# Gate columns as the stationary operand, the delta rule's output in two groups of four, and the stream 192 bytes further along

## The chip, the cores and the metric

The kernel runs on one core of one Trainium2 chip. The metric is device microseconds of one execution. Three runs of the kernel before took 1904.73, 1896.8 and 1905.82 us, so the median is 1904.73 us. Every profile row further down is from one more, profiled execution.

## The reference, cut to what matters

A model of four blocks works on one sequence of 256 tokens of width 1024, all in float32: two blocks of the first kind (L = 0, 1), then two of the second kind (L = 2, 3). The change touches the first kind alone, and there the mixer called the gated delta rule. From the reference:

```python
proj = h @ w_in
(dn_qkv, dn_z, dn_b, dn_a, ...) = jnp.split(proj, ...)   # dn_b, dn_a: 4 columns each
beta = jax.nn.sigmoid(dn_b)
g = -jnp.exp(dn_A_log) * jax.nn.softplus(dn_a + dn_dt_bias)

def step(state, inp):                   # one of 4 chunks of 64 tokens, 4 heads at once
    u_c, w_c, a_c, qd_c, kt_c, dl_c = inp
    v_new = u_c - jnp.einsum('bhck,bhkv->bhcv', w_c, state)
    o = jnp.einsum('bhck,bhkv->bhcv', qd_c, state) + jnp.einsum('bhcj,bhjv->bhcv', a_c, v_new)
    state = state * dl_c[..., None, None] + jnp.einsum('bhck,bhcv->bhkv', kt_c, v_new)
    return state, o
```

`h` is the RMS norm of the stream, so `dn_b` and `dn_a` are eight columns of the product of the stream with `w_in`, times one factor for each token. The output `o` of a chunk is the sum of two products for each head: one with the state, one with `v_new`. In the first chunk the state is zero and the first product falls away.

## The kernel before, in words

**Weights and the big products.** All weights come as 572 chunks of 128 partitions by 1024 columns. SyncE issues each chunk's DMA into a ring `raw`; ScalarE casts it to its high part `whi` (line 636); VectorE subtracts to get its low part `wlo` (line 1126, as part of `split`; GpSimd does some). The three rings hold four chunks each. The stream lies in two tiles: `hh` is its high part and `hl` its low part, each eight blocks of 256 tokens. A product of one weight block of 128x128 with the stream is three matmuls with 256 moving columns, `hh` with `whi`, `hl` with `whi` and `hh` with `wlo` (helper `mm3`). A chunk of `w_in` is 24 such matmuls. All matmuls are recorded at line 2001, in the helper `mm`; operands read in plain float32 need two passes each, shown as two records.

**The start of a block.** `first(L)` on TensorE opens with `project("qkv", L, ...)`, a generator that does one chunk for each `next`. In its hook, between chunk 3 and chunk 4 (counted from 0; the order's rows and the timeline show it behind a chunk in bank 5), it issues `norm_sum`, two plain float32 matmuls that sum squares; from these ScalarE makes `RSB`, the norm's factor along the free axis, and VectorE makes `RST`, the same factor with tokens on the partitions. After chunk 4 TensorE issues the gate columns: `SW` holds the eight columns of `w_in` for `dn_b` and `dn_a`, as 8 high and 8 low columns for each of eight blocks. ScalarE fills the high half (line 882) and VectorE the low half in their own hooks. The product goes to bank 1 with tokens on the partitions; VectorE copies the low half out (line 1451), adds the high half, and multiplies by `RST`. Then `beta` and the decays follow in a few 128x8 instructions of both engines. Beside this VectorE runs, for every chunk of qkv, one `wlo`, and for most of them one multiplication by `RSB` that empties a bank (128x512) and six steps of the convolution.

**The delta rule beside the weights.** `mixers` and `run` interleave the delta rule's steps with weight chunks of the same block (`fill`): a step of the small matmuls, one chunk, the next step. `delta(L)` writes the output of chunk n = 0..3, for heads of each half, into banks 2 and 3 by matmuls with 64 moving columns: `St` (the state, 128 rows by 128 columns) for n > 0 and `VN` (the new values, 64 rows by 128 columns). In the trace a name such as 64*128 ahead of the shape is the part of the array that the stationary operand fills: rows by columns. The four heads run in a loop, each with its `St` matmul and then its `VN` matmul. Ahead of them, in the same step, stand four matmuls of 64 rows (two passes each) for the state. There are two blocks with n = 0, and three with `St` in each of the two layers: six.

**Addresses.** The tiles lie one behind the other in the local memory: rings first, then constants, parameters, `small`, `RST`, then `hh`, `hl`, `RSB`, `SW` and the big `region` that holds nearly every other tile (`area`).

Of the kernel before, what the change touches and what calls it, by code (L numbers as in the profile page):

```python
# [7 lines left out]
F32 = mybir.dt.float32  # L8
# [47 lines left out]
                         ("dnout", 1), ("retout", 4), ("pscale", 4), ("alog", 8), ("dtb", 8)])  # L56
N_PAR2 = _columns(PAR2, [("attn", 8), ("mlp", 8), ("final", 8), ("idxk", 1), ("sinks", 8)])
N_PAR = DEPTH * (N_PAR1 + N_PAR2)
N_SMALL = 64 + 512


class Job:
# [120 lines left out]
def wide(ap, axis, n):  # L183

    shape = list(ap.shape)
    shape.insert(axis, n)
    return ap.unsqueeze(axis).broadcast_to(shape)
# [84 lines left out]
def program(nc, ins, out):  # L272
    with ExitStack() as ctx:
# [35 lines left out]
        def sb(name, shape, dt=F32, offset=None):  # L309
            n = 4  # L310
            for x in shape[1:]:
                n *= x
            if offset is None:
                offset = at[0]
                at[0] += (n + 31) // 32 * 32
            return nc.alloc_sbuf_tensor_at(name, shape, dt, offset=offset)
# [5 lines left out]
        cst = sb("cst", [P, N_CONST])  # L322
        par = sb("par", [P, N_PAR])
        small = sb("small", [P, N_SMALL])
        RST = sb("RST", [P, 2])
        hh = sb("hh", [P, 8, T], F32R)
        hl = sb("hl", [P, 8, T], F32R)
        RSB = sb("RSB", [P, T])
        SW = sb("SW", [P, 8, 16], F32R)
        region = at[0]  # L330
        nslots = (nc.sbuf_usable_end - region) // 4096
        assert nslots >= 30, nslots
        area = nc.alloc_sbuf_tensor_at("area", [P, 30 * 1024], F32, offset=region)

        def slot(i, n=1):
# [60 lines left out]
        a_, be, g_, eg, kx = (SM[:, 16 * i:16 * i + 8] for i in (0, 1, 2, 4, 5))  # L396
        G_, GL = SM[:, 48:56], SM[:, 56:64]
        u1, u2 = SM[:, 128:136], SM[:, 144:152]
        AB2, tmp2 = (SM[:, c:c + 16].rearrange("p (s c) -> p s c", s=2) for c in (192, 224))
        AB = SM[:, 192:208].rearrange("p (s c) -> p c s", s=2)  # L400
        sm3 = small[:, 0:64].rearrange("p (k c) -> p k c", c=8)

        QF = slot(0, 7)
# [208 lines left out]
        def scalar(a):  # L612
# [246 lines left out]
            def first(L):  # L859
# [18 lines left out]

                def hook():
                    factor(norm)  # L880
                    a.wait_ge(s_small[L], 16)
                    a.copy(SW[:, :, 0:8], sm3).then_inc(*a_dn.up("SW", L))

                def rv(m0):
                    a.wait_ge(*v_norm.at("turned", norm))
# [2 lines left out]
                qkv = project("qkv", L, conv, hook)  # L888
                next(qkv)
                next(qkv)  # L890
                next(qkv)
                next(qkv)
                a.wait_ge(*v_dn.at("ab", L))
# [230 lines left out]
        def vector(v):  # L1124
            def tt(dst, x, y, op):
                return v.tensor_tensor(dst, x, y, op)  # L1126
# [291 lines left out]
            def first(L):  # L1418
# [19 lines left out]

                def hook():
                    factor(norm)  # L1440
                    v.wait_ge(*a_dn.at("SW", L))
                    tt(SW[:, :, 8:16], sm3, SW[:, :, 0:8].bitcast(F32), OP.subtract).then_inc(*v_dn.up("SW", L))

                qkv = project("qkv", L, conv, hook, norm)
                next(qkv)
                next(qkv)
                next(qkv)
                next(qkv)
                two = bank[1][:, 0:32].rearrange("p (s c) -> p s c", s=2)
                v.wait_ge(*e_dn.at("ab", L))  # L1450
                v.tensor_copy(tmp2, two[:, :, 8:16]).then_inc(*v_dn.up())
                v.wait_ge(*v_dn.now())
                tt(AB2, two[:, :, 0:8], tmp2, OP.add).then_inc(*v_dn.up("absum", L))
                v.wait_ge(*v_dn.now())
                v.wait_ge(*v_norm.at("turned", norm))
                tt(AB2, AB2, wide(RST[:, :], 2, 8), OP.mult).then_inc(*v_dn.up("ab", L))
                v.wait_ge(*v_dn.now())

                dn = delta(L)
# [530 lines left out]
        def tensor(e):  # L1990
# [9 lines left out]
            def mm(ps, x, y, start, stop, skip=False):  # L2000
                return e.matmul(ps, x, y, start=start, stop=stop, skip_group_check=skip)  # L2001
# [248 lines left out]
            def fresh2(b0, event):  # L2250
                for j in range(2):
                    fresh(b0 + j, event(j))

            def delta(L):
# [74 lines left out]
                for n in range(4):  # L2329
# [18 lines left out]
                    if n == 0:  # L2348
                        e.wait_ge(*g_dn.at("q", L))
                        fresh2(2, lambda j: a_dn.at("OD", L, j))  # L2350
                    for h in range(4):
                        b = 2 * h + half
                        o = bank[2 + h // 2][:, 256 * (h % 2) + 64 * n:256 * (h % 2) + 64 * n + 64]
                        if n:
                            mm(o, St[:, 128 * h:128 * h + 128], Aq[:, 256 * h + 64 * n:256 * h + 64 * n + 64], True, False)
                        x = mm(o, hv(VN)[r, h, :], AT[r, 128 * b + 64 * q:128 * b + 64 * q + 64], n == 0, True)
                    x.then_inc(*e_dn.up("o", L, n))
                    yield 1
                e.wait_ge(*a_dn.at("square", L))
# [89 lines left out]
            def first(L):  # L2449
# [9 lines left out]
                next(qkv)  # L2459
                next(qkv)  # L2460
                next(qkv)
                next(qkv)
                e.wait_ge(*v_dn.at("SW", L))
                fresh(1, v_dn.at("absum", L))
                for s in range(2):
                    for k in range(8):
                        mm(bank[1][:, 16 * s:16 * s + 16], hh[:, k, 128 * s:128 * s + 128], SW[:, k, :], k == 0, False, True)
                        x = mm(bank[1][:, 16 * s:16 * s + 8], hl[:, k, 128 * s:128 * s + 128], SW[:, k, 0:8], False, k == 7, True)
                x.then_inc(*e_dn.up("ab", L))
                dn = delta(L)  # L2470
                next(dn)
# [282 lines left out]
def parameters(inputs):  # L2754
# [4 lines left out]
    for l in range(DEPTH):  # L2759
# [17 lines left out]
        put(PAR2, par2, "sinks", x["sinks_2"][l].reshape(2, 2, 2).transpose(0, 2, 1).reshape(1, 8))  # L2777
        small[l][:, 0:64] = x["w_in"][l][:, 2048:2056].reshape(8, P, 8).transpose(1, 0, 2).reshape(P, 64)
        small[l][:, 64:576] = x["pool_w"][l].transpose(1, 0, 2).reshape(P, 512)
    return par1, par2, small  # L2780


# [32 lines left out]
```

## Time and profile before

| what | value |
|---|---|
| median of three runs | 1904.73 us |
| the profiled execution's own time | 1908.99 us |
| its span | 1907.2 us |
| mean granted TensorE clock | 0.993 |
| TensorE busy (PE) | 1879.3 us, 99% |
| VectorE busy (DVE) | 1246.2 us, 65% |
| ScalarE busy (ACT) | 955.7 us, 50% |
| GpSimd busy (POOL) | 308.5 us, 16% |
| chain that ended last | PE 90%, DVE 7%, ACT 1%, DMA 1% |

Busy shares are of the whole span, and the chain's shares tell which engine the end waited for. A granted clock of 1.00 is 2.4 GHz on TensorE, one of 0.50 is 1.2 GHz; a mean between them is a stretch with some of each.

### The profile page before, as it was taken

How to read it: one execution, taken by the hardware profiler on the slowest of the kernel's cores; microseconds unless marked ns; L12 is line 12 of the kernel's file. 1: busy time of each engine (PE TensorE's matmuls, PEld its weight loads, DVE VectorE, ACT ScalarE, POOL GpSimd, SP SyncE). 2: the span in 40 equal slices, each digit the busy share in tenths (PEclk: the TensorE clock that was granted, in tenths of full speed). 3: DMA queues.
4: the chain of work that ended last, by engine and by line, in shares of the span. 5: the costliest groups of instructions: out<-in, count | busy, mean ns of one | idle time of the engine just before them, and what ended most of it. 6: DMA issues, size and time to landing. Idle time of an engine off the chain costs nothing.

```text
span 1907.2 us, 36402 instructions
## 1 busy us (share of the span) xinstructions
PE 1879.3 (99%) x15460; PEld 1791.1 (94%) x15460; DVE 1246.2 (65%) x1678; ACT 955.7 (50%) x1381; POOL 308.5 (16%) x176
## 2 busy tenths in 40 slices
PE   7999999999999999999999999999999999999998
PEld 7989998998899999999989999999999899999998
DVE  6884567665689545877658775577547684677643
ACT  5633456544563435564445445555534444556533
POOL 0050231000003203200002342320001352321000
PEclk9999999999999999999999999999999999999999
DMA  6443344655445323555565553355555663345553
GB/s 228 161 145 111 120 146 159 211 187 198 145 154 178 110 97 127 200 181 182 193 209 184 178 179 131 123 188 193 187 186 179 211 195 121 132 167 188 190 187 100
DMA packets 92161, 317.59 MB, mean 167 GB/s; under 512 B 11744, under 2 KB 12896, under 8 KB 91744
## 3 DMA queue, kind: packets, MB, share of 16 engines
q1 hardware_dynamic: 91424, 314.69, 48.9%
q8 instruction: 123, 2.02, 0.4%
q10 hardware_dynamic: 576, 0.57, 0.1%
q14 instruction: 38, 0.31, 0.0%
HBM read 304.99 MB, written 1.05 MB: 160 GB/s over the span
## 4 chain that ended last, share of the span: by engine, by line
PE 90%; DVE 7%; ACT 1%; DMA 1%; issue 1%; SPq 0%; DVEq 0%; ACTq 0%
PE bank L2001 89%; DVE wlo L1126 3%; DVE area L1126 2%; PE bank L2543 1%; DVE area L1132 1%; DMA raw<-in_weights 1%; DVE hl L1132 1%; DVE xT L1132 1%; ACT area L630 1%; ACT whi L636 0%; PE bank L2561 0%; PE bank L2220 0%; DVE area L1196 0%; DVE xT L1126 0%; DVE area L1645 0%
## 5 line engine op out<-in xcount | busy, mean ns | idle before, releaser
L1126 DVE TENSOR_TENSOR wlo<-raw,whi 128x1024 fp32r<-128x1024 f32 x518 | 659.9, 1289 | 399.1 <-ACT whi L636 398.6
L2001 PE MATMUL bank<-hh,whi 128*128 128x256 f32 x2928 | 835.3, 286 | 15.8 <-DVE wlo L1126 13.1
L2001 PE MATMUL bank<-hh,wlo 128*128 128x256 f32 x2928 | 818.6, 281 | 0.0
L2001 PE MATMUL bank<-hl,whi 128*128 128x256 f32 x2928 | 811.7, 281 | 0.0
L636 ACT CAST whi<-raw 128x1024 fp32r<-128x1024 f32 x572 | 589.0, 1046 | 412.3 <-PE bank L2001 361.2
L2001 PEld LDWEIGHTS bank<-hh,whi 128*128 128x128 f32 x2928 | 555.7, 190 | 30.0 <-DVE wlo L1126 14.7
L2001 PEld LDWEIGHTS bank<-hl,whi 128*128 128x128 f32 x2928 | 555.8, 191 | 1.9 <-issue 1.9
L2001 PEld LDWEIGHTS bank<-hh,wlo 128*128 128x128 f32 x2928 | 556.2, 190 | 0.0
L1781 POOL TENSOR_TENSOR area<-area 128x512 f32<-128x512 f32 (+4 forms) x86 | 137.4, 1604 | 559.3 <-ACT area L630 219.4
L1781 POOL TENSOR_TENSOR wlo<-raw,whi 128x1024 fp32r<-128x1024 f32 x54 | 134.0, 2483 | 426.3 <-ACT whi L636 426.3
L2001 PE MATMUL bank<-area 64*64 64x64 f32 (+7 forms) x1928 | 184.9, 268 | 0.7 <-DVE area L1196 0.7
L2001 PEld LDWEIGHTS bank<-area 64*64 64x64 f32 (+3 forms) x1928 | 163.9, 168 | 18.3 <-issue 6.9
L2001 PE MATMUL bank<-FH,whi 128*128 128x256 f32 x640 | 180.1, 281 | 0.0
L2001 PE MATMUL bank<-FL,whi 128*128 128x256 f32 x640 | 179.6, 281 | 0.0
L2001 PE MATMUL bank<-FH,wlo 128*128 128x256 f32 x640 | 179.6, 281 | 0.0
L630 ACT ACTIVATE area<-area 128x256 f32<-128x256 f32 (+8 forms) x247 | 140.7, 578 | 50.6 <-DVE area L1132 18.6
L2001 PEld LDWEIGHTS bank<-FL,whi 128*128 128x128 f32 x640 | 122.3, 191 | 0.1
L2001 PEld LDWEIGHTS bank<-FH,whi 128*128 128x128 f32 x640 | 120.1, 188 | 0.4 <-issue 0.3
L2001 PEld LDWEIGHTS bank<-FH,wlo 128*128 128x128 f32 x640 | 120.5, 188 | 0.0
L1126 DVE TENSOR_TENSOR area<-bank,area 128x512 f32<-128x512 f32 (+4 forms) x146 | 83.0, 610 | 42.9 <-PE bank L2001 39.5
L1126 DVE TENSOR_TENSOR area<-bank,RSB 128x512 f32<-128x512 f32 (+1 forms) x118 | 80.2, 682 | 44.1 <-PE bank L2001 41.4
L2001 PE MATMUL bank<-wlo,FH 128*128 128x512 f32 x240 | 94.8, 395 | 0.0
(129 smaller groups left out, 1915.5 us busy)
## 6 DMA issues: line engine op xcount, KB each, us to landing
raw<-in_weights SPq DMA_DIRECT2D x572, 512.0 KB, 4.1
area<-area SPq DMA_DIRECT2D x96, 64.0 KB, 3.5
area<-area SPq DMA_DIRECT2D x16, 128.0 KB, 3.8
cst<-in_const SPq DMA_DIRECT2D x1, 1188.0 KB, 7.3
cst<-in_const SPq DMA_DIRECT2D x1, 1024.5 KB, 5.5
xT<-in_x SPq DMA_DIRECT2D x4, 256.0 KB, 8.0
out<-xT SPq DMA_DIRECT2D x4, 256.0 KB, 2.9
area<-in_lev SPq DMA_DIRECT2D x2, 384.0 KB, 6.6
```

The costliest lines, as they stand in the source:

```text
L630: return a.activation(dst, src, fn, scale=scale, **more)
L636: a.copy(whi[:, i % RING, :], raw[:, i % RAW, :]).then_inc(*hi.up(i))
L1126: return v.tensor_tensor(dst, x, y, op)
L1132: return v.scalar_tensor_tensor(out=dst, in0=x, scalar=s, in1=y, op0=op0, op1=op1)
L1781: return g.tensor_tensor(dst, x, y, op)
L2001: return e.matmul(ps, x, y, start=start, stop=stop, skip_group_check=skip)
L2543: o = e.transpose(bank[b][:, 128 * u:128 * u + 128], x.grid()[:, j % 2, j // 2, 128 * kb:128 * kb + 128], C("eye"))
```

## The change: what it does

**Gate columns.** `SW` becomes the stationary operand and the stream the moving one: 16 matmuls (8 blocks, one with `hh` and 16 columns of `SW`, one with `hl` and 8) with 256 moving columns, instead of 32 with 16 or 8. They stand behind `norm_sum` and ahead of chunk 4. The result has the eight columns on partitions 0 to 15 and tokens along the free axis. VectorE copies it (16x256) to `ABR`. After chunk 4 TensorE turns it back with two plain float32 matmuls against a small matrix of two stacked 8x8 identities, which comes with `small` and also adds the high and low halves. VectorE then needs one instruction, the multiplication by `RST`, where it had three. The cast and the subtraction that fill `SW` move one weight chunk earlier on ScalarE and VectorE.

**Output.** For n > 0 the four `St` matmuls stand ahead of the four `VN` matmuls.

**Addresses.** `small` grows by 32 bytes for each partition, `RST` moves behind the region, and a gap is put in, so that `hh`, `hl`, `RSB`, `SW` and the region begin 192 bytes further along in each partition. The rings keep their addresses.

The diff, with unchanged lines left out:

```diff
-N_SMALL = 64 + 512
+N_SMALL = 64 + 512 + 8
...
-        RST = sb("RST", [P, 2])
+        at[0] += 192
         hh = sb("hh", [P, 8, T], F32R)
...
-        nslots = (nc.sbuf_usable_end - region) // 4096
+        at[0] += 30 * 4096
+        RST = sb("RST", [P, 2])
...
+        ABR = SM[0:16, 0:256]
...
@@ ScalarE, first block
                 def hook():
                     factor(norm)
-                    a.wait_ge(s_small[L], 16)
-                    a.copy(SW[:, :, 0:8], sm3).then_inc(*a_dn.up("SW", L))
...
                 next(qkv)
                 next(qkv)
+                a.wait_ge(s_small[L], 16)
+                a.copy(SW[:, :, 0:8], sm3).then_inc(*a_dn.up("SW", L))
...
@@ VectorE, first block
                 def hook():
                     factor(norm)
-                    v.wait_ge(*a_dn.at("SW", L))
-                    tt(SW[:, :, 8:16], sm3, SW[:, :, 0:8].bitcast(F32), OP.subtract).then_inc(*v_dn.up("SW", L))
+                    v.wait_ge(*e_dn.at("abrow", L))
+                    v.tensor_copy(ABR, bank[1][0:16, 0:256]).then_inc(*v_dn.up("abrow", L))
...
                 next(qkv)
                 next(qkv)
+                v.wait_ge(*a_dn.at("SW", L))
+                tt(SW[:, :, 8:16], sm3, SW[:, :, 0:8].bitcast(F32), OP.subtract).then_inc(*v_dn.up("SW", L))
                 next(qkv)
                 next(qkv)
-                two = bank[1][:, 0:32].rearrange("p (s c) -> p s c", s=2)
                 v.wait_ge(*e_dn.at("ab", L))
-                v.tensor_copy(tmp2, two[:, :, 8:16]).then_inc(*v_dn.up())
-                v.wait_ge(*v_dn.now())
-                tt(AB2, two[:, :, 0:8], tmp2, OP.add).then_inc(*v_dn.up("absum", L))
-                v.wait_ge(*v_dn.now())
                 v.wait_ge(*v_norm.at("turned", norm))
-                tt(AB2, AB2, wide(RST[:, :], 2, 8), OP.mult).then_inc(*v_dn.up("ab", L))
+                tt(AB2, bank[1][:, 256:272].rearrange("p (s c) -> p s c", s=2), wide(RST[:, :], 2, 8), OP.mult).then_inc(*v_dn.up("ab", L))
...
@@ TensorE, delta
+                    def place(h):
+                        return bank[2 + h // 2][:, 256 * (h % 2) + 64 * n:256 * (h % 2) + 64 * n + 64]
+                    if n:
+                        for h in range(4):
+                            mm(place(h), St[:, 128 * h:128 * h + 128], Aq[:, 256 * h + 64 * n:256 * h + 64 * n + 64], h % 2 == 0, False, True)
                     for h in range(4):
                         b = 2 * h + half
-                        o = bank[2 + h // 2][:, 256 * (h % 2) + 64 * n:256 * (h % 2) + 64 * n + 64]
-                        if n:
-                            mm(o, St[:, 128 * h:128 * h + 128], Aq[:, 256 * h + 64 * n:256 * h + 64 * n + 64], True, False)
-                        x = mm(o, hv(VN)[r, h, :], AT[r, 128 * b + 64 * q:128 * b + 64 * q + 64], n == 0, True)
+                        x = mm(place(h), hv(VN)[r, h, :], AT[r, 128 * b + 64 * q:128 * b + 64 * q + 64], n == 0, True, True)
...
@@ TensorE, first block
                 next(qkv)
+                e.wait_ge(*v_dn.at("SW", L))
+                fresh(1, v_dn.at("ab", L))
+                for k in range(8):
+                    mm(bank[1][0:16, 0:T], SW[:, k, :], hh[:, k, :], k == 0, False, True)
+                    x = mm(bank[1][0:8, 0:T], SW[:, k, 0:8], hl[:, k, :], False, k == 7, True)
+                x.then_inc(*e_dn.up("abrow", L))
                 next(qkv)
-                e.wait_ge(*v_dn.at("SW", L))
-                fresh(1, v_dn.at("absum", L))
+                e.wait_ge(*v_dn.at("abrow", L))
                 for s in range(2):
-                    for k in range(8):
-                        mm(bank[1][:, 16 * s:16 * s + 16], hh[:, k, 128 * s:128 * s + 128], SW[:, k, :], k == 0, False, True)
-                        x = mm(bank[1][:, 16 * s:16 * s + 8], hl[:, k, 128 * s:128 * s + 128], SW[:, k, 0:8], False, k == 7, True)
+                    x = mm(bank[1][:, T + 8 * s:T + 8 * s + 8], ABR[:, 128 * s:128 * s + 128], small[0:16, 576:584], True, True)
                 x.then_inc(*e_dn.up("ab", L))
...
+        small[l][0:16, 576:584] = np.tile(np.eye(8, dtype=np.float32), (2, 1))
```

How the instructions move, at the three places that matter. In these rows a matmul's names are bank<-stationary and moving tile in the order of the alphabet, and the shape is that of its output; the number at a name tells tiles apart. First TensorE behind `norm_sum`, which is the row with `cst`, before:

```order
L2001 MATMUL bank5<-hh_57,wlo_52 128x256
L2001 MATMUL bank0<-area_61,cst_53 128x128 x2
L2001 MATMUL bank6<-hh_57,whi_51 128x256
L2001 MATMUL bank6<-hl_58,whi_51 128x256
L2001 MATMUL bank6<-hh_57,wlo_52 128x256
...
L2001 MATMUL bank1<-SW_60,hh_57 128x16
L2001 MATMUL bank1<-SW_60,hl_58 128x8
```

and after:

```order
L2002 MATMUL bank5<-hh_56,wlo_52 128x256
L2002 MATMUL bank0<-area_61,cst_53 128x128 x2
L2002 MATMUL bank1<-hh_56,SW_59 16x256
L2002 MATMUL bank1<-hl_57,SW_59 8x256
...
L2002 MATMUL bank1<-small_55,area_61 128x8 x2
```

The gate columns moved from behind chunk 4 (bank 6) to ahead of it, and their output lies turned; only the two small matmuls stay behind chunk 4. Next VectorE at the same place, before:

```order
L1126 TENSOR_TENSOR wlo<-raw,whi 128x1024 x3
L1126 TENSOR_TENSOR area<-RSB,cst 128x256
L1190 TENSOR_REDUCE RST<-area 128x2
L1126 TENSOR_TENSOR SW<-small,SW 128x8x8
L1126 TENSOR_TENSOR area<-bank,RSB 128x512 x2
...
L1126 TENSOR_TENSOR wlo<-raw,whi 128x1024
L1451 COPY area<-bank 128x16
L1126 TENSOR_TENSOR area<-bank,area 128x16
L1126 TENSOR_TENSOR area<-area,RST 128x16
L1126 TENSOR_TENSOR area<-area,par 128x8
```

and after:

```order
L1130 TENSOR_TENSOR wlo<-raw,whi 128x1024 x2
L1130 TENSOR_TENSOR SW<-small,SW 128x8x8
L1130 TENSOR_TENSOR wlo<-raw,whi 128x1024
L1130 TENSOR_TENSOR area<-RSB,cst 128x256
L1194 TENSOR_REDUCE RST<-area 128x2
L1446 COPY area<-bank 16x256
L1130 TENSOR_TENSOR area<-bank,RSB 128x512 x2
...
L1130 TENSOR_TENSOR wlo<-raw,whi 128x1024
L1130 TENSOR_TENSOR area<-bank,RST 128x16
L1130 TENSOR_TENSOR area<-area,par 128x8
```

The subtraction moved one `wlo` earlier, the new copy stands in its old place, and two of three small instructions are gone. Last the output step of the delta rule on TensorE in layer 0 with n > 0 (banks 2 and 3 take the outputs, bank 1 the state's part), before:

```order
L2001 MATMUL bank1<-area_61 128x128 x4
L2001 MATMUL bank2<-area_61 128x64 x4
L2001 MATMUL bank3<-area_61 128x64 x4
L2001 MATMUL bank6<-hh_57,whi_51 128x256
```

and after:

```order
L2002 MATMUL bank1<-area_61 128x128 x4
L2002 MATMUL bank2<-area_61 128x64 x2
L2002 MATMUL bank3<-area_61 128x64 x2
L2002 MATMUL bank2<-area_61 128x64 x2
L2002 MATMUL bank3<-area_61 128x64 x2
L2002 MATMUL bank6<-hh_56,whi_51 128x256
```

The same eight matmuls: before, `St` and `VN` by turns within each row of four; now the first two rows are `St` and the last two `VN`.

## Rows read from the trace of the kernel before

**Rows 1.** The page: busy time; the chain that ended last; a group (count | busy, mean ns).

```profile
PE 1879.3 (99%) x15460; PEld 1791.1 (94%) x15460; DVE 1246.2 (65%) x1678; ACT 955.7 (50%) x1381; POOL 308.5 (16%) x176
PE 90%; DVE 7%; ACT 1%; DMA 1%; issue 1%; SPq 0%; DVEq 0%; ACTq 0%
...
L2001 PE MATMUL bank<-hh,whi 128*128 128x256 f32 x2928 | 835.3, 286 | 15.8 <-DVE wlo L1126 13.1
```

**Rows 2.** The chain in order of time: start us, length us, what.

```profile
20.00 48.48 PE bank L2001 x375
...
149.90 66.78 PE bank L2001 x540
...
554.48 1.24 DVE wlo L1126
...
618.17 17.15 PE bank L2001 x220
```

**Rows 3.** Stretches, TensorE: us, PE busy (records), granted clock, DMA share, GB/s.

```profile
27.98:31.88 3.90, 3.90 (x34) 0.89 1.00 402
31.88:37.79 5.91, 5.91 (x29) 0.50 0.36 119
528.54:532.03 3.49, 3.49 (x34) 1.00 0.30 119
532.03:536.03 4.00, 4.00 (x23) 0.60 0.41 137
```

**Rows 4.** TensorE's timeline, both layers' norm_sum: start us, length us, engine, line, operation.

```profile
24.71 0.60 PE L2001 MATMUL bank<-area,cst 128*128 128x128 f32 x4
...
525.64 0.35 PE L2001 MATMUL bank<-hh,whi 128*128 128x256 f32 x1 [0.66 <-DVE wlo L1126]
```

**Rows 5.** VectorE's timeline, same columns, layer 0 and then layer 1.

```profile
26.77 0.42 DVE L1190 TENSOR_REDUCE RST<-area 128x2 f32<-128x256 f32 x1
27.10 0.22 DVE L1126 TENSOR_TENSOR SW<-small,SW 128x64 fp32r<-128x64 f32 x1
...
32.56 0.17 DVE L1451 COPY area<-bank 128x16 f32<-128x16 f32 x1
32.77 0.17 DVE L1126 TENSOR_TENSOR area<-bank,area 128x16 f32<-128x16 f32 x1
...
37.38 0.69 DVE L1126 TENSOR_TENSOR area<-bank,RSB 128x512 f32<-128x512 f32 x1 [0.76 <-PE bank L2001]
...
45.22 0.68 DVE L1126 TENSOR_TENSOR area<-bank,RSB 128x512 f32<-128x512 f32 x1
...
51.35 0.68 DVE L1126 TENSOR_TENSOR area<-bank,RSB 128x512 f32<-128x512 f32 x1
...
55.20 2.36 DVE L1126 TENSOR_TENSOR wlo<-raw,whi 128x1024 fp32r<-128x1024 f32 x2 [0.30 <-ACT whi L636]
...
536.67 0.69 DVE L1126 TENSOR_TENSOR area<-bank,RSB 128x512 f32<-128x512 f32 x1 [0.37 <-PE bank L2001]
```

**Rows 6.** Stretches, TensorE: output steps and what follows them.

```profile
165.97:167.89 1.92, 1.92 (x17) 1.00 0.61 203
174.87:179.62 4.75, 4.75 (x25) 0.81 0.29 110
179.62:184.88 5.26, 5.26 (x25) 0.52 0.27 90
188.83:192.83 4.00, 4.00 (x26) 1.00 0.36 128
690.00:692.00 2.00, 2.00 (x11) 0.50 0.00 0
692.00:694.00 2.00, 2.00 (x13) 0.69 0.42 137
```

**Rows 7.** Stretches, TensorE: two stretches of 40 us at full clock.

```profile
400.00:440.00 40.00, 40.00 (x342) 1.00 0.55 185
900.00:940.00 40.00, 40.00 (x355) 1.00 0.57 191
```

More of the change, by code:

```diff
@@ L330, in program @@
         region = at[0]
-        nslots = (nc.sbuf_usable_end - region) // 4096
-        assert nslots >= 30, nslots
+        at[0] += 30 * 4096
+        RST = sb("RST", [P, 2])
+        assert at[0] <= nc.sbuf_usable_end, at[0]
         area = nc.alloc_sbuf_tensor_at("area", [P, 30 * 1024], F32, offset=region)
@@ L398, in program @@
         u1, u2 = SM[:, 128:136], SM[:, 144:152]
-        AB2, tmp2 = (SM[:, c:c + 16].rearrange("p (s c) -> p s c", s=2) for c in (192, 224))
+        AB2 = SM[:, 192:208].rearrange("p (s c) -> p s c", s=2)
         AB = SM[:, 192:208].rearrange("p (s c) -> p c s", s=2)
+        ABR = SM[0:16, 0:256]
         sm3 = small[:, 0:64].rearrange("p (k c) -> p k c", c=8)
```

## The prediction, made before the changed kernel ran

> **What bounds the kernel now.** I read the page first. TensorE is busy for 99% of the span, and the chain that ended last runs over it for 90% and over VectorE for 7% [rows 1]. So work taken from TensorE is worth its length where the chain lies on TensorE, and nothing where it lies on VectorE. The chain in order of time says which is where [rows 2]. The output steps of the delta rule lie between 165 and 204 us and between 674 and 702 us, inside chain pieces of TensorE (149.90 to 216.68 in layer 0, and from 618.17 on in layer 1). There each microsecond counts. In the qkv product the chain is named as TensorE from 20.00 to 68.48, but this needs a second look: in layer 1 at the same place it goes over a `wlo` of VectorE at 554.48. In layer 0 the same `wlo` pair starts at 55.20 and takes 2.36 us [rows 5], so its first half ends at about 56.4, and TensorE takes the chunk that needs it at about that time. Both engines arrive together there, and whichever is faster gains nothing alone.
>
> Third, the granted clock. Behind the gate columns it fell to half: 0.50 over 5.91 us in layer 0, 0.60 over 4.00 us in layer 1 [rows 3]. It also fell behind two of the six output steps: 0.81 and 0.52 over 4.75 and 5.26 us, and 0.50 and 0.69 over two times 2 us [rows 6]. The loss in a stretch is its length times one minus its clock. That gives 0.43 + 2.96 = 3.4 us and 1.6 us for the gate columns, and 0.90 + 2.52 = 3.4 us and 1.0 + 0.62 = 1.6 us behind the output steps: 10.0 us in all.
>
> **The gate columns on TensorE.** Before: 32 matmuls. In layer 1, at full clock, they took 3.49 us [rows 3], 0.109 us each although they move only 16 or 8 columns; so the 128-column load of `hh` or `hl` sets the pace. After: 16 matmuls with 256 moving columns. At 40/355 = 0.113 us each [rows 7] this is 1.8 us. A stationary tile of 16 columns is a new shape; entering and leaving one costs, and two float32 matmuls (four passes, about 0.11 each) follow chunk 4. I add 0.9 us. So TensorE's own work falls by 3.5 − 2.7 = 0.8 us, and with the half clock gone by 0.8 + 3.4 = 4.2 us in layer 0 and 0.8 + 1.6 = 2.4 us in layer 1. In layer 1 the new block also fills time in which TensorE sat idle: 0.66 us ahead of chunk 4 [rows 4], which makes 3.1 us. I expect the clock to stay up because what preceded the fall is gone: 3.5 us of matmuls that are nearly all loading. What I can't exclude is that it falls anyway.
>
> The Trainium skill, in "TensorE: Matmul & The Clock Gate", section "LDWEIGHTS (loading the stationary operand)", says that a load takes columns divided by 1.2 ns, 107 ns for 128. The trace agrees: 109 ns in a run of matmuls that move next to nothing [rows 3]. By it the new loads of 16 columns would be 13 ns, and the 256 moving columns alone would set the pace, as my 1.8 us has it.
>
> **The gate columns on VectorE, which decides what of this is paid out.** From 38 us on VectorE is in a loop: two chunks in 51.35 − 45.22 = 6.13 us [rows 5], against 48 x 0.113 = 5.4 us on TensorE. TensorE has no lead to spend; if it comes earlier it waits for `wlo`. So what counts is by how much VectorE's loop starts earlier. Its wait for TensorE's bank, 0.76 us in layer 0 and 0.37 us in layer 1, goes, since chunk 4 and the next come earlier. Two small instructions go: 32.77 − 32.56 = 0.21 us each, 0.42. The `SW` subtraction moves into a time where VectorE waits anyway (behind the `wlo` of that chunk it has nothing to do until ScalarE's `RSB` comes), and in its place stands the new copy of 16x256. No row shows this shape. Its bounds: 0.17 us (a copy of 128x16) and 0.42 us (the reduction with 256 columns, both [rows 5]), against 0.22 us for the subtraction that leaves; I take 0.35, nearer to the row with the same 256 columns, so 0.13 to 0.2 us more than before. The copy must wait for the 16 matmuls. `norm_sum` starts at 24.71 [rows 4] and its four passes are through by 25.1, so they end at 25.1 + 2.0 = 27.1 us, and the reduction ahead of the copy ends at 27.2, so no new wait, but only by a tenth. In layer 1 the room is larger, since the block starts while chunk 4 still waits. Sum: layer 0 0.76 + 0.42 − 0.25 = 0.93 us, layer 1 0.37 + 0.42 − 0.2 = 0.59 us; together **1.5 us**. Its bounds are 0 (the copy waits and eats it) and 4.2 + 3.1 = 7.3 us (VectorE doesn't bind after all). Behind qkv the float chain of `beta` has only become shorter.
>
> **The output steps.** One with `St` takes 4.00 us for 24 records of its own at full clock; the one without `St` (n = 0) takes 1.92 us for 16 [rows 6]. The 8 more passes at 0.109 us are 0.87 us; the other 2.08 − 0.87 = 1.21 us are what the eight changes between a tile of 128 rows and one of 64 rows cost, 0.15 us each. Grouped there are two changes instead of eight: 6 x 0.15 = 0.9 us for a step, and six steps make **5.4 us**; I take 5.3, rounded down because the changes between matmuls of one step may hide a little in each other. It is in chain pieces of TensorE, and VectorE and ScalarE have idle time there. Bounds: 0 (the change of bank or of tile costs the same as the change of rows) and 6 x 1.21 = 7.3 us.
>
> The Trainium skill, in "TensorEngine Tiling (Array Packing)", section "Tiling Modes", says that changing the mode drains TensorE while changing the tile doesn't. The trace agrees, with 0.15 us for a change. The rule would put the same price on the new 16-column block, which I have in the 0.9 us above.
>
> **The clock behind the output steps.** It fell behind two of six steps in this execution and cost 5.0 us. The steps become a fifth shorter and denser. That can spare the falls, or none, or put one elsewhere. I take half, **2.5 us**, with bounds of 0 and 5.0.
>
> **Addresses.** No row shows what 192 bytes do. From below and above I take what the trace has at one clock for the same instructions: 342 matmul records in 40 us in one stretch and 355 in another [rows 7], 0.117 and 0.1127 us each, 4%. I take 0 and keep this for a rival. The Trainium skill, in "SBUF — State Buffer", section "Specifications (TRN2)", gives lines of 16 bytes, and 192 is twelve of them, so by that rule nothing changes; no run here shows it yet.
>
> **The sum.** 1.5 + 5.3 + 2.5 = 9.3 us from 1908.99 us gives 1899.7. The median of the runs is 4.3 us below the profiled execution, and the lowest 12 us. I suppose that a median run has lost less by half clock, so that only 1.3 of the 2.5 us can be saved there: 1904.73 − 1.5 − 5.3 − 1.3 = 1896.6. I say 1896.5.
>
> **Rivals.**
> 1. VectorE doesn't bind in qkv, or all falls of the clock go: the full 7.3 us in qkv, or 5.3 + 1.5 + 5.0. From the median 6.8 + 5.8 or 6.8 + 5.0, about 1892. For it: TensorE is called the chain in all of 20.00 to 68.48 [rows 2]. Against it: the period of 6.13 us.
> 2. Only the six steps pay, and the falls of the clock come back elsewhere: 5.3 or less, about 1900. For it: the two falls behind output steps came at only two of six like places, so what sets them off isn't just the step itself. In that case the clock would also fall in qkv, behind other work.
> 3. The order of the outputs saves nothing, because a new stationary tile costs the same whichever its rows: 1904.73 − 1.5 − 1.3, about 1902. Against it: n = 0 has 16 passes in 1.92 us, each with a tile of its own.
> 4. Slower: TensorE's pace for 256 moving columns depends on where the stream lies. The same matmul has two paces in this trace. There are 3 x 2928 of them with the stream's tiles [rows 1], about 8,800; if a third of all ran at 0.117 where they now run at 0.1127, it would be 2930 x 0.0043 = 12.6 us, and 1904.73 − 8.1 + 12.6 = 1909; with a half, 1915.5. It decides from about 1900 matmuls on, which is 8.1/0.0043. For it: the two paces are there at one clock. Against it: both are there with one placement, so placement alone does not set them.
>
> **Chances.** The forecast 0.42, rival 1 0.20, rival 2 0.20, rival 3 0.07, rival 4 0.11. The likeliest alone spans 1893 to 1900. The range reaches to rival 1 with a run-to-run spread of some microseconds below it, and to rival 3 above: 1887 to 1906. About 0.5%, 9.5 us, is what a measurement can tell here; that is below 1895.2 and above 1914.3. Rival 1 and half of the forecast's width lie below: 0.40. Of rival 4 about 0.08 lies above. The rest is 0.52.
>
> **What would show it.** Right: 16 records with a stationary of 16 columns right behind `norm_sum`, in about 2 us; a clock of 1.00 from 25 to 40 us and from 525 to 540 us; VectorE without a wait for TensorE's bank near 37 us, its next loop starting 0.9 us (0.6 us in layer 1) earlier; TensorE with small waits for `wlo` between 40 and 56 us; output steps of 3.1 us instead of 4.00. Wrong: VectorE waiting for the new copy's matmuls; TensorE a full 4 us ahead at 68 us; output steps that still take 4 us; or 40 us stretches whose record counts differ from 342 and 355 at places that the change doesn't touch, which would be rival 4.

## The result, and the profile after

The changed kernel took 1927.76 us, the median of four runs from 1927.51 to 1930.07 us; the kernel before took 1905.28 us, the median of four from 1896.8 to 1909.77. The ratio is 1.0115, with a 95% interval of 1.0082 to 1.0148: some 22 us slower, where 8 us faster were forecast. The profiled execution took 1927.51 us against 1908.99. One later run of the kernel before, among those made beside the first address experiments, took 2311.37 us against 1892 to 1915 us for the other 18, and the ratios there leave it out.

The page after, in the same lines as [rows 1]: busy time, the chain that ended last, and the costliest group of matmuls.

```profile
PE 1897.3 (99%) x15436; PEld 1808.5 (94%) x15436; DVE 1250.8 (65%) x1676; ACT 957.1 (50%) x1381; POOL 303.7 (16%) x176
...
PE 90%; DVE 6%; ACT 2%; DMA 1%; issue 1%; SPq 0%; DVEq 0%; ACTq 0%
...
L2002 PE MATMUL bank<-hh,whi 128*128 128x256 f32 x2928 | 839.8, 288 | 16.3 <-DVE wlo L1130 12.8
```

TensorE is busy for 18 us more, with 24 records fewer, so it takes longer over what it had before. The mean duration of a matmul on the page hardly shows it (288 against 286 ns), since matmuls are pipelined. The distance between their starts shows it. Here are two starts that lie 24 matmuls apart, in the middle of a long stretch at full clock, first of the kernel before and then of the changed one (timeline: start us, length us, engine, operation):

```profile
909.79 0.28 PE L2001 MATMUL bank<-hh,whi 128*128 128x256 f32 x1
...
912.51 0.28 PE L2001 MATMUL bank<-hh,whi 128*128 128x256 f32 x1
```

```profile
909.79 0.28 PE L2002 MATMUL bank<-hh,whi 128*128 128x256 f32 x1
...
912.64 0.28 PE L2002 MATMUL bank<-hh,whi 128*128 128x256 f32 x1
```

That is 2.72/24 = 113.3 ns before and 2.85/24 = 118.8 ns after. The place shown ran at the faster of two paces before. The kernel has 11,748 matmuls with 256 moving columns and 128x128 weights. Over the whole trace, the starts of successive ones lie 116.0 ns apart in the mean before, in two paces, about two fifths at 113.3 and three fifths at 117.8 ns. After, they lie 118.9 ns apart, most at 118.7 and about a quarter at 120.0 ns. So both kernels have two paces, and in the changed one both are slower.

What the change was forecast to do where it was made, it did. TensorE's and then VectorE's timeline after, layer 0:

```profile
23.34 0.61 PE L2002 MATMUL bank<-area,cst 128*128 128x128 f32 x4
23.70 0.36 PE L2002 MATMUL bank<-hh,SW 128*16 128x256 f32 x1
...
25.65 0.28 PE L2002 MATMUL bank<-hh,whi 128*128 128x256 f32 x1
```

```profile
25.40 0.42 DVE L1194 TENSOR_REDUCE RST<-area 128x2 f32<-128x256 f32 x1
25.85 0.41 DVE L1446 COPY area<-bank 16x256 f32<-16x256 f32 x1
...
35.06 0.68 DVE L1130 TENSOR_TENSOR area<-bank,RSB 128x512 f32<-128x512 f32 x1
...
52.86 2.36 DVE L1130 TENSOR_TENSOR wlo<-raw,whi 128x1024 fp32r<-128x1024 f32 x2 [0.30 <-ACT whi L640]
```

The 16 matmuls take 25.65 − 23.70 = 1.95 us, the copy 0.41, and the wait of 0.76 us for TensorE's bank [rows 5] is gone at 35.06. The stretches of TensorE (us, PE busy, granted clock, DMA share, GB/s), three output steps and the places where the clock had fallen [rows 3, 6]:

```profile
174.60:177.76 3.16, 3.16 (x26) 1.00 0.52 166
184.85:188.00 3.15, 3.15 (x26) 1.00 0.48 160
195.10:198.26 3.16, 3.16 (x26) 1.00 0.54 167
30.00:40.00 10.00, 10.00 (x86) 1.00 0.56 203
170.00:190.00 20.00, 20.00 (x158) 1.00 0.31 103
530.00:540.00 10.00, 10.00 (x85) 1.00 0.32 107
680.00:700.00 20.00, 20.00 (x158) 1.00 0.40 132
```

All six output steps fell to 3.16 us, from 4.00 at full clock, and at the places where the clock had fallen it now stays full. So where is the loss? The chain after, in order of time, has it at two marks:

```profile
552.11 1.24 DVE wlo L1130
...
616.73 17.34 PE bank L2002 x220
```

At 616.73 us the changed kernel is still 1.44 us ahead of [rows 2] (618.17). Then one and the same small block of the third layer, before and after:

```profile
1101.69 1.26 PE L2001 MATMUL bank<-area 64*128 64x128 f32 x12
```

```profile
1106.07 1.26 PE L2002 MATMUL bank<-area 64*128 64x128 f32 x12
```

It is 4.38 us behind there and 1925.7 − 1907.2 = 18.5 us behind at the end. Those last 14 us arise in a part of the program in which the change has not one instruction. Only the addresses differ there.

### The profile page after: what moved, and what is told of

Read it like the earlier page. It is cut to its first block, busy times and chain, and to the rows that moved or that the text cites. A ratio compares the mean times of both kernels' runs of the same rounds, so it can differ in the third digit from the quotient of the medians.

```text
span 1925.7 us, 36352 instructions
## 1 busy us (share of the span) xinstructions
PE 1897.3 (99%) x15436; PEld 1808.5 (94%) x15436; DVE 1250.8 (65%) x1676; ACT 957.1 (50%) x1381; POOL 303.7 (16%) x176
## 4 chain that ended last, share of the span: by engine, by line
PE 90%; DVE 6%; ACT 2%; DMA 1%; issue 1%; SPq 0%; DVEq 0%; ACTq 0%
PE bank L2002 89%; DVE wlo L1130 2%; DVE area L1130 1%; ACT area L634 1%; PE bank L2554 1%; DVE area L1136 1%; DVE hl L1136 1%; DVE xT L1136 1%; ACT whi L640 1%; DMA xT<-in_x 0%; DMA raw<-in_weights 0%; DVE area L1646 0%; PE bank L2221 0%; DVE area L1644 0%; PE bank L2572 0%
## 5 line engine op out<-in xcount | busy, mean ns | idle before, releaser
L2002 PEld LDWEIGHTS bank<-hl,whi 128*128 128x128 f32 x2928 | 548.9, 189 | 1.9 <-issue 1.9
L1782 POOL TENSOR_TENSOR area<-area 128x512 f32<-128x512 f32 (+4 forms) x86 | 132.9, 1550 | 569.5 <-ACT area L634 224.3
L2002 PE MATMUL bank<-area 64*64 64x64 f32 (+7 forms) x1928 | 179.2, 267 | 0.7 <-DVE area L1200 0.7
L1130 DVE TENSOR_TENSOR area<-bank,area 128x512 f32<-128x512 f32 (+3 forms) x144 | 82.6, 615 | 46.8 <-PE bank L2002 42.4
```

Of the source, the lines that this page charges most:

```text
L1782: return g.tensor_tensor(dst, x, y, op)
```

## The experiments

**Four parts, one by one.** All four ran on one chip beside 29 runs of the kernel before (median 1911.09 us).

The changed kernel without its gap:

```diff
-        at[0] += 192
         hh = sb("hh", [P, 8, T], F32R)
```

> The changed kernel with the gap of 192 bytes taken out, so that stream, SW and region lie where they lay before; gate columns and output order as changed. Placement theory (TensorE's pace for 256 moving columns is set by where the moving tiles lie): the paces of before come back (342 to 355 records in the 40 us stretches from 400 and from 900 us, against 340 and 339 in the changed kernel), and the time is the one before less 1.5 us in qkv, 5.0 us for the output steps and up to 10 us of half clock: 1889 to 1899 us. History theory (the new instructions themselves, by their order, leave TensorE in the slower pace): it stays within 3 us of 1927.8 us.

Measured: ratio to the kernel before 0.9964 (0.9939 to 0.9990), median 1904.51 us of 12 runs from 1886.85 to 1908.38. In its profiled execution (1886.85 us, the fastest) the mean pace is 115.2 ns and the clock is 0.999. Its counts in the 40 us stretches were 336 and 293, not the 342 to 355 expected. That says nothing of the pace: this execution is so far ahead that 19 and 62 of the matmuls in these stretches are others, with 512 moving columns and about 230 ns each, and the rest start 113.3 ns apart. From here on I read starts. The median lies above the 1889 to 1899 us expected, and the kernel before was slower on this chip too (1911.09 us for 1905.28). The rest of the change is a gain of 0.36%, and the gap turned it into a loss.

The kernel before with the gap alone:

```diff
+        at[0] += 192
         hh = sb("hh", [P, 8, T], F32R)
```

> The kernel before with nothing but a gap of 192 bytes ahead of the stream. Placement theory: about 11,400 matmuls take 119 instead of 116 ns each, so 33 us more, 1938 us, or down to 1928 if the falls to half clock go as they did in the changed kernel; 340 records or fewer in each 40 us stretch. History theory: no change, 1900 to 1909 us.

Measured: 1.0173 (1.0138 to 1.0208), median 1941.27 us; 1.0173 of 1905 is 33 us more. Two starts 24 matmuls apart:

```profile
909.77 0.28 PE L2002 MATMUL bank<-hh,wlo 128*128 128x256 f32 x1
...
912.65 0.28 PE L2002 MATMUL bank<-hh,wlo 128*128 128x256 f32 x1
```

2.88/24 = 120.0 ns; the mean of the trace is 119.2. That is what the placement theory said, within some 3 us (the medians differ by 30 us, the ratio makes 33), and the history theory (no change) falls.

The output steps alone:

```diff
+                    if n:
+                        for h in range(4):
+                            mm(place(h), St[...], Aq[...], h % 2 == 0, False, True)
                     for h in range(4):
                         b = 2 * h + half
-                        o = bank[2 + h // 2][...]
-                        if n:
-                            mm(o, St[...], Aq[...], True, False)
-                        x = mm(o, hv(VN)[r, h, :], AT[...], n == 0, True)
+                        x = mm(place(h), hv(VN)[r, h, :], AT[...], n == 0, True, True)
```

> The kernel before with only the output steps regrouped (St four times, then VN four times). Both theories: each of the six steps takes 3.16 us instead of 4.00, 5.0 us less in all, and no change of pace; 1900 us, or down to 1895 if the falls to half clock behind output steps go too. If the history theory holds in the form that the order of outputs matters for what follows, the pace behind these steps turns to 0.119 us and the time rises to 1915 or more.

Measured: 0.9963 (0.9936 to 0.9989), median 1899.82 us: 7 us less. And the gate columns alone (the diff is the changed kernel's, without the part on `place` and without the gap):

> The kernel before with only the gate columns as the stationary operand; output steps and addresses as before. Placement theory: 0.9 us in layer 0 and 0.6 us in layer 1 from VectorE's earlier loop, and the clock stays up behind the gate columns; since VectorE binds there, this pays nothing more: 1903.8 us, or down to 1898 if the falls behind the output steps go as well. History theory: the new block leaves TensorE in the slower pace, 1915 us or more.

Measured: 1.0005 (0.9979 to 1.0031), median 1912.01 us: no gain that can be told, and the 1.5 us expected are too small for this interval to show or exclude. Stretches of TensorE, of the gate columns alone and then of the output steps alone:

```profile
170.00:180.00 10.00, 10.00 (x65) 0.86 0.23 73
180.00:190.00 10.00, 10.00 (x64) 0.80 0.30 106
190.00:200.00 10.00, 10.00 (x53) 0.66 0.16 53
690.00:700.00 10.00, 10.00 (x65) 0.83 0.15 52
30.00:40.00 10.00, 10.00 (x89) 1.00 0.55 199
```

```profile
30.00:40.00 10.00, 10.00 (x75) 0.83 0.57 202
520.00:530.00 10.00, 9.34 (x71) 0.87 0.57 185
170.00:180.00 10.00, 10.00 (x82) 1.00 0.30 105
180.00:190.00 10.00, 10.00 (x81) 1.00 0.30 107
690.00:700.00 10.00, 10.00 (x79) 1.00 0.33 109
```

With the new gate columns the clock stays up behind them and falls behind output steps, for 1.4 + 2.0 + 3.4 + 1.7 = 8.5 us in this one execution, more than in the profile before (5.0). With the new output steps the falls behind them are gone, and those behind the gate columns stay, smaller than before (3.4 us for 5.0); by the prediction's argument VectorE's loop hides most of their cost, which no run tests. One execution is little to go by, since the falls differ from run to run. Over all runs the mean clock is 0.9943 for the kernel before (29 runs), 0.9957 with the gate columns alone, 0.9966 with the output steps alone, and 0.9987 with both (12 runs each). So with the gate columns alone a part of what they save may come back behind output steps, and the two gains of clock together (0.0014 + 0.0023) are most of what both parts bring (0.0044). Only with both parts is it 0.998 or 0.999 in all 12 runs.

**Whose address counts?** These two ran on one chip together with the gaps of 64 and 128 bytes further down (median before 1906.81 us). First the 192 bytes ahead of the rings, so that rings and stream move together:

```diff
+        at[0] += 192
         raw = sb("raw", [P, RAW, 1024])
...
-        at[0] += 192
         hh = sb("hh", [P, 8, T], F32R)
```

> The changed kernel, but the 192 bytes are put ahead of the weights' rings, so that rings, constants, stream and region all lie 192 bytes further and no distance between them differs from before. If what counts is how the moving tile lies relative to the stationary one (distance theory), TensorE has the two paces of before, 113.3 and 117.8 ns, and the time is that of the changed instructions at the old addresses, 1887 to 1908 us, median 1904. If the moving tile's own address counts (own-address theory), the matmuls keep their mean of 119 ns and the time is 1925 to 1930 us.

Measured: 0.9941 (0.9910 to 0.9972), median 1895.44 us. Two starts 24 matmuls apart:

```profile
909.80 0.28 PE L2002 MATMUL bank<-hh,whi 128*128 128x256 f32 x1
...
912.52 0.28 PE L2002 MATMUL bank<-hh,whi 128*128 128x256 f32 x1
```

113.3 ns again, with the stream at the very address at which the changed kernel had it. So the distance between stream and weights counts, not the stream's own place. Next the gap behind `SW`, for the region alone (one run):

```diff
-        at[0] += 192
         hh = sb("hh", [P, 8, T], F32R)
...
+        at[0] += 192
         region = at[0]
```

> The changed kernel with the gap of 192 bytes behind SW: only the region (with FH and FL, the moving tiles of w_down, 1920 matmuls of 256 columns) lies further, the stream hh and hl where it lay before. Both placement theories: matmuls with hh and hl have the paces 113.3 and 117.8 ns, those with FH and FL 119 to 120; so about 1920 x 2 to 3 ns = 4 to 6 us more than with no gap, 1891 to 1910 us. If the region alone did it (through other engines' tiles in it), all matmuls take 119 ns and the time is 1927 us.

Measured: 1906.7 us. Counted over the whole trace, matmuls with `hh` and `hl` as the moving tile come 115.6 ns apart, in the paces 113.3 and 117.8; those with `FH` and `FL` come 118.7 ns apart. Each class follows its own tile. One run of a kernel whose fellows spread over 20 us says nothing by its time; the paces do, and they exclude that the region's place slows all matmuls.

**The distance, step by step.** Only the number in `at[0] += 192` was changed. The gaps of 256, 32 and 224 bytes ran on a third chip (median before 1902.38 us). The rings' tiles begin at multiples of 256 bytes, so the last bits of `hh`'s address are the distance modulo 256.

> The changed kernel with a gap of 64 bytes in place of 192. Placement theory with a pattern that repeats: hh begins at 88064, which is 0 modulo 256, as the rings do; no trace so far shows this residue. If equal residues of moving and stationary tile are the bad case, and 192 (residue 128) is only half bad, it is slower than 1928 us, up to 1950. If the farther from the residue of before (192) the worse, then 64 lies between: 1905 to 1928. If only lines of 16 bytes counted, it would be as with no gap, 1887 to 1908.

> The changed kernel with a gap of 128 bytes in place of 192; hh begins at 88128, residue 64 modulo 256. By symmetry with the residue of before (192 and 64 lie equally far from the rings' residue 0) the two paces of before would come back: 1887 to 1908 us. If each step of 64 bytes from the old place only makes it worse, it is at 1920 to 1928.

> The changed kernel with a gap of 256 bytes in place of 192: the stream lies again 192 bytes, modulo 256, behind the rings, as before. Distance theory with a period of 256 bytes: the paces 113.3 and 117.8 ns come back and the time with them, 1887 to 1908 us. If the period is longer (512 or more) or the distance itself counts, the pace stays at 118 to 120 ns and the time is 1915 to 1935 us.

> The changed kernel with a gap of 32 bytes: residue 224 of 256, between those of no gap (192) and of a gap of 64 (0, every matmul at 120.0 ns). If the pattern goes in steps of 64 bytes, it is like one of its neighbours: 1887 to 1908 us or 1934. If it changes smoothly, between: 1910 to 1925. Lines of 16 bytes alone would give no difference from no gap.

> The changed kernel with a gap of 224 bytes: residue 160 of 256, between that of the changed kernel (128, 1928 us) and of no gap (192, 1887 to 1908 us). Steps of 64 bytes: as at 192, 1928 us, or as with no gap. Smooth: between, 1905 to 1920 us, with matmuls of 115 to 118 ns.

| gap, bytes | distance mod 256 | ratio to before | 95% interval | mean pace, profiled run |
|---|---|---|---|---|
| 0 | 192 | 0.9964 | 0.9939 to 0.9990 | 115.2 ns |
| 32 | 224 | 1.0081 | 1.0056 to 1.0106 | 118.3 ns |
| 64 | 0 | 1.0126 | 1.0090 to 1.0162 | 119.9 ns |
| 128 | 64 | 1.0038 | 1.0018 to 1.0058 | 117.5 ns |
| 192 (the change) | 128 | 1.0115 | 1.0082 to 1.0148 | 118.9 ns |
| 224 | 160 | 1.0089 | 1.0060 to 1.0119 | 118.2 ns |
| 256 | 192 | 0.9951 | 0.9917 to 0.9985 | 115.7 ns |
| 192, rings too | 192 | 0.9941 | 0.9910 to 0.9972 | 115.4 ns |

Gaps of 0 and 256 agree, so the pattern repeats after 256 bytes. Distance 0 is the slowest of these, as one of the expectations had it. Distance 64 came out at 117.5 ns: nearly always the slower of the two paces that 192 has, so my "by symmetry" was half right. The gaps of 32 and 224 bytes give 118.3 and 118.2 ns. That is at no neighbour's value, so the step form is out. Both lie between their neighbours, nearer to the slower one: gap 32 came out inside the smooth form's range (1922.11 us of 1910 to 1925), gap 224 just outside it (1921.80 us of 1905 to 1920).

The profiled executions of the eight placements in the table tie pace to time. A straight line through them, from 115.2 ns and 1886.85 us to 119.9 ns and 1935.09 us, rises by 10.4 us for each nanosecond, and none lies more than 3 us off it. All 11,748 matmuls on the critical path would make 11.7 us for each.

**TensorE alone.** To measure the disputed cost by itself:

```diff
+ORDER = [p for _ in range(5) for k in range(8) for p in ((k, k), (k, 8 + k), (8 + k, k))]
...
+            x = [e.matmul(bank[1][:, 0:T], st(k, 0), mv(j, 192), start=i == 0, stop=i == 119, skip_group_check=True) for i, (k, j) in enumerate(ORDER)][-1]  # stationary 0, moving 192
+            x.then_inc(s_pe, 1)
+            e.wait_ge(s_v, 2)
```

> A kernel that computes nothing of the model: after one copy of x into a stationary tile S and a moving tile M, TensorE alone runs 38 blocks of 120 matmuls (128x128 stationary, 256 moving, float32r, in the order high-high, high-low, low-high), each pair of blocks at another start address of M, with S at 0 or 64 modulo 256; between blocks VectorE copies one bank, nothing else runs and no transfer is under way. Distance theory (TensorE's own two reads, of the stationary and of the moving tile, get in each other's way, by the distance of their addresses modulo 256): a block at distance 192 takes 120 x 113.3 to 117.8 ns = 13.6 to 14.1 us, at 0 it takes 120 x 120 = 14.4, at 64 14.1, at 128 14.2 to 14.4, at 32, 160 and 224 between; and with S at 64, M at 0 behaves as 192 did and M at 64 as 0. Rival (other engines' or transfers' accesses to the same memory slow TensorE down): with nothing beside it, every block takes the same, 13.6 us or less. Rival (own address of the moving tile counts): with S at 64 the blocks behave by M's residue as with S at 0.

The timeline, one block of 120 matmuls to a row (start us, length us). In order: distances 192, 224, 0, 64 twice, 128, 192 once more twice; then, with the stationary tile at 64, the moving tile at 0 and at 64.

```profile
53.90 13.88 PE L325 MATMUL bank<-M,S 128*128 128x256 f32 x120 [0.52 <-DVE xT L308]
68.30 14.47 PE L328 MATMUL bank<-M,S 128*128 128x256 f32 x120 [0.52 <-DVE xT L308]
98.26 14.66 PE L334 MATMUL bank<-M,S 128*128 128x256 f32 x120 [0.52 <-DVE xT L308]
...
158.18 13.87 PE L346 MATMUL bank<-M,S 128*128 128x256 f32 x120 [0.52 <-DVE xT L308]
172.57 14.40 PE L349 MATMUL bank<-M,S 128*128 128x256 f32 x120 [0.52 <-DVE xT L308]
...
217.83 14.50 PE L358 MATMUL bank<-M,S 128*128 128x256 f32 x120 [0.52 <-DVE xT L308]
...
277.77 13.89 PE L370 MATMUL bank<-M,S 128*128 128x256 f32 x120 [0.52 <-DVE xT L308]
292.17 14.40 PE L373 MATMUL bank<-M,S 128*128 128x256 f32 x120 [0.52 <-DVE xT L308]
...
456.67 13.89 PE L406 MATMUL bank<-M,S 128*128 128x256 f32 x120 [0.52 <-DVE xT L308]
...
485.47 14.64 PE L412 MATMUL bank<-M,S 128*128 128x256 f32 x120 [0.52 <-DVE xT L308]
```

No other engine works during a block, and transfers are at 1 GB/s or less. Still the same differences come out: 14.66 − 13.88 = 0.78 us for 120 matmuls between distances 0 and 192, or 6.5 ns each, against 119.9 − 113.3 = 6.6 ns in the full kernel. A block's length holds its slower start too. In its middle the starts lie 113.3 ns apart at 192, 118.3 at 224, 120.0 at 0, 118.7 at 128, and 113.3 or 117.8 at 64: the full kernel's paces. With the stationary tile at 64 the two values change places as the distance says: the moving tile at 0 now takes 13.89 us and at 64 it takes 14.64. Both rivals, other engines' accesses and the moving tile's own address, are out as what sets these paces. And the same distance, 192 as well as 64, gave 13.9 us in one block and 14.4 in another. The output bank isn't what differs: at 192 the blocks at 53.90 and 292.17 us both write bank 4. Distances 160, 208 and 16 had two lengths as well (14.51 and 14.35, 14.56 and 14.27, 14.51 and 14.27 us), and distance 96, which no full kernel had, was as slow as 0 (14.65 us). So the pace doesn't follow the distance in a smooth line. This kernel ran once.

## Why the prediction was wrong

**The step that failed is the one on addresses: "I take 0 and keep this for a rival".** Its cost is 33 us when it is alone (1.0173), and 1.0115/0.9964 = 1.0152, or 29 us, beside the other parts. Rival 4 had the right mechanism (TensorE's pace depends on where the stream lies) and a price of 12.6 to 19 us. That was too low, because it counted only a share of the matmuls turning from the fast pace of before to its slow one; in fact nearly all went to paces that the trace of before does not have, 118.7 and 120.0 ns. It also counted 3 x 2928 matmuls, those with `hh` and `hl`, where some 11,700 of this form had their moving tile shifted. Its own evidence was misread too. I held against it that both paces appear with one placement, so that placement alone doesn't set them. That is true, and it excluded nothing: placement sets which paces there are, and something else picks between two of them. Rows 7, read as a bound, gave the difference within one distance and no bound for another distance.

The Trainium skill was used for the same step ("SBUF — State Buffer", section "Specifications (TRN2)", lines of 16 bytes, of which 192 bytes are a whole number). The measurement decides against that use, that a shift by whole lines changes nothing: gaps of 32, 64 and 128 bytes are whole numbers of such lines as well, and they moved the time by 0.7 to 1.6% against no gap. In "TensorE: Matmul & The Clock Gate", section "Step-by-step: what each phase is for", it also says that loading the next tile's weights takes no read bandwidth from the running matmul. TensorE alone doesn't fit that: its pace changes by up to 6.5 ns a matmul with the distance between the two tiles. That the two reads get in each other's way is the reading I take; the runs show the dependence on the distance and not what happens inside.

**The gate columns on TensorE: right.** 1.95 us for the 16 matmuls, where 1.8 was said, and the clock stayed up, here and with the gate columns alone.

**What VectorE pays out: right, nearly to the digit.** From the instruction that reads `RSB` to the `wlo` pair that TensorE then waits for it was 55.20 − 26.31 = 28.89 us in layer 0 and is 52.86 − 24.94 = 27.92; in layer 1 554.48 − 525.97 = 28.51 and now 552.11 − 524.18 = 27.93. That is 0.97 + 0.58 = 1.55 us, forecast 1.5. The new copy took 0.41 us, not 0.35, and found its matmuls done.

**The output steps: right in kind, a little large.** 6 x 0.84 = 5.0 us against 5.3.

**The clock behind them: under-valued, and its cause not seen.** Half of the falls behind output steps were forecast to go. In the profiles of seven of the eight placements with both parts all went, in that at a gap of 64 bytes one was left (a clock of 0.83 from 680 to 690 us). With the gate columns alone they went behind these and grew behind the output steps, which is like rival 2; with the output steps alone they went behind these and stayed in part behind the gate columns. In time the parts add up as far as this can be told: 0.9963 x 1.0005 = 0.9968 alone, 0.9964 together, each with about 0.0026 either way. The argument that took 1.3 us for the 2.5, that a median run of the kernel before has lost less by half clock, is not borne out: of 29 runs the fastest (1893.37 us) and the slowest (1917.83) both have a mean clock of 0.993.

**The sum without the gap: right, and in part by luck.** The forecast was 8.1 us below the median, 0.43%; the change without its gap measured 0.36% (0.10 to 0.61). Three placements of the changed kernel at distance 192 beat both kernels, at 0.9941 to 0.9964. But the interval reaches from 2 to 12 us, and the terms didn't come out as summed: 1.55 + 5.0 us for the instructions, and up to 5.0 us behind the output steps where 1.3 was taken.

**What stays open.** What picks between the two paces of one distance wasn't tried: 113.3 and 117.8 ns at 192 and 64, in the full kernel also 118.7 and 120.0 at 128. It is no small matter: in 12 runs of the kernel without the gap, at a clock of 0.998 or 0.999 throughout, the time spread from 1886.85 to 1908.38 us, while at distance 128 four runs lay within 2.6 us and at 0 four within 2.5. I take the spread for this choice in the main. For it: the three profiled executions of the changed instructions at distance 192 took 1886.85, 1890.12 and 1895.42 us at mean paces of 115.2, 115.4 and 115.7 ns. It was not tested by itself.

## What to carry to other kernels

Where TensorE loads new 128x128 float32r weights for every matmul of 256 moving columns, the address of the moving tile relative to the stationary one, modulo 256 bytes, is a size of its own, worth up to 6.5 ns in 120. No distance is best for every form: the 1,008 matmuls here that have the stream as the stationary tile and 512 columns of weights moving were fastest at distance 0, where the 256-column ones were slowest. So count matmuls before calling a change of layout free, and when a change moves tiles, undo the move first. Read the pace from starts many matmuls apart, not from durations, nor from counts of records in a fixed stretch, which may hold other work in another execution. Where falls of the clock are part of the gain, compare mean clocks over many runs, not one profile of each.

## What the runs showed of the hardware

- The pace of 128x128 float32r weights with 256 moving columns at full clock, TensorE alone, 120 matmuls: 13.88 us at distance 192, 14.66 at 0, 14.65 at 96, 14.50 at 128, 14.47 at 224, 14.27 at 32; at 192 and at 64 both 13.9 and 14.4 us, at 192 with the same output bank.
- With the roles exchanged (stream stationary, weights with 512 columns moving), the starts in the full kernel lie 230.2 ns apart before (`hh` at 192 modulo 256), 232.5 in the changed kernel (128), 227.1 with a gap of 64 bytes (0) and 233.3 with one of 128 (64).
- A change between stationary tiles of 128 and 64 rows costs about 0.84/6 = 0.14 us each, an estimate: six such changes fewer took an output step from 4.00 to 3.16 us, with the output steps alone as well, where nothing else was changed.
- A block of 16-column stationary tiles with 256 moving columns ran at 1.95/16 = 0.122 us a matmul with its entry, no faster than the 256-column matmuls with 128-column weights (0.113 to 0.120 us).
